# Gated one-hot rows from two ScalarE operations a token, three dense products beside each 16 tokens, and all sparse dots inside the chunks

## The reference

```python
q = (xt @ w_query).reshape(t, PEER_HEADS, 2, D_HALF)
scores = jnp.einsum('thpd,hpnd->thpn', q, sub_keys)
sv, si = lax.top_k(scores, PEER_TOPK)                  # 16 of 128, for each half of the key
...
top_s, pos = lax.top_k(cand_s, PEER_TOPK)              # 16 of the 256 sums
idx = jnp.take_along_axis(cand_i, pos, axis=-1)
gate = jax.nn.softmax(top_s, axis=-1)
...
a = jnp.einsum('ted,td->te', jnp.take(expert_u, ii, axis=0), xi)
w = gi * jax.nn.gelu(a)
y = jnp.einsum('te,ted->td', w, jnp.take(expert_v, ii, axis=0))
```

## Time and profile before

| what | value |
|---|---|
| median of the runs | 1685.22 us (1684.25 to 1688.5) |
| profiled execution | 1689.51 us, span 1687.8 us |
| mean granted TensorE clock | 0.982 |
| PE / DVE / ACT / POOL busy | 1587.2 / 1258.3 / 664.9 / 391.9 us |
| moved by DMA | 426.26 MB |

### The profile page before, as it was taken

How to read it: one execution, slowest core, us unless ns; L and a number is a source line. 1 busy time by engine, 2 the same in 40 slices (tenths; PEclk the granted TensorE clock), 3 DMA queues, 4 the chain that set the end, 5 groups by cost and what they waited for, 6 DMA issues and landing times.

```text
span 1687.8 us, 22615 instructions
## 1 busy us (share of the span) xinstructions
PE 1587.2 (94%) x7605; PEld 1292.7 (77%) x7605; DVE 1258.3 (75%) x2268; ACT 664.9 (39%) x1227; POOL 391.9 (23%) x326
## 2 busy tenths in 40 slices
PE   1899988999999999999989999799999999999995
PEld 0454465554559999999989999798888888888884
DVE  6448364439957987899788988558888878788887
ACT  2111132221337852588336853233333333333333
POOL 1101400000002320033001346413344334334420
PEclk9989989999999999999999999999999999999998
DMA  9765420000127994489736999987999999999982
GB/s 361 275 229 181 149 76 0 1 0 1 50 85 278 363 360 150 160 325 357 278 135 224 361 387 413 402 314 261 367 352 345 354 357 354 329 362 359 344 315 87
DMA packets 172770, 426.26 MB, mean 253 GB/s; under 512 B 13068, under 2 KB 62220, under 8 KB 169496
## 3 DMA queue, kind: packets, MB, share of 16 engines
q1 hardware_dynamic: 86400, 265.89, 42.2%
q0 software_dynamic: 36864, 134.23, 21.8%
q10 hardware_dynamic: 49432, 25.19, 5.3%
HBM read 372.84 MB, written 52.43 MB: 252 GB/s over the span
## 4 chain that ended last, share of the span: by engine, by line
PE 87%; DVE 6%; DMA 3%; ACT 2%; issue 1%; ACTq 1%; SPq 0%; DVEq 0%
PE bank L1152 10%; PE bank L1153 10%; PE bank L1156 10%; PE bank L1097 10%; PE bank L1099 10%; PE bank L1098 10%; PE bank L1043 7%; PE bank L951 5%; PE bank L1112 5%; PE bank L1026 3%; PE bank L961 3%; PE bank L921 1%; DMA weights<-in_w_ada 1%; PE bank L1053 1%; ACTq L842 1%
## 5 line engine op out<-in xcount | busy, mean ns | idle before, releaser
L1097 PE MATMUL bank<-h_hi,u_hi 128*128 128x384 f32 x1024 | 350.7, 343 | 22.0 <-DVE u_lo L1490 13.2
L1098 PE MATMUL bank<-h_lo,u_hi 128*128 128x384 f32 x1024 | 345.0, 337 | 0.0
L1099 PE MATMUL bank<-h_hi,u_lo 128*128 128x384 f32 x1024 | 345.0, 337 | 0.0
L1152 PE MATMUL bank<-v_hi,w_hi 128*128 128x512 f32 x768 | 299.2, 390 | 1.7 <-DVE w_lo L1597 1.6
L1153 PE MATMUL bank<-v_lo,w_hi 128*128 128x512 f32 x768 | 298.8, 389 | 0.0
L865 ACT ACTIVATE v_hi<-weights 128x1024 fp32r<-128x1024 f32 x128 | 135.8, 1061 | 330.2 <-PE bank L1156 264.3
L1156 PE MATMUL bank<-v_hi,w_lo 128*128 128x512 f32 x768 | 236.4, 389 | 0.0
L1593 DVE TENSOR_TENSOR v_lo<-weights,v_hi 128x1024 fp32r<-128x1024 f32 x128 | 157.7, 1232 | 95.2 <-ACT v_hi L865 93.0
L1490 DVE TENSOR_TENSOR u_lo<-weights,u_hi 128x1024 fp32r<-128x1024 f32 x128 | 155.9, 1223 | 95.8 <-PE bank L1099 72.7
L1097 PEld LDWEIGHTS bank<-h_hi,u_hi 128*128 128x128 f32 x1024 | 194.7, 190 | 25.3 <-DVE u_lo L1490 12.8
L1098 PEld LDWEIGHTS bank<-h_lo,u_hi 128*128 128x128 f32 x1024 | 194.8, 190 | 0.0
(11 more groups left out here) (233 smaller groups left out, 2179.6 us busy)
## 6 DMA issues: line engine op xcount, KB each, us to landing
weights<-in_uT SPq DMA_DIRECT2D x128, 512.0 KB
weights<-in_expert_v SPq DMA_DIRECT2D x128, 512.0 KB, 7.8
weights<-in_w_ada SPq DMA_DIRECT2D x12, 2048.0 KB, 10.3
gates_dense<-weights SPq DMA_DIRECT2D x24, 1024.0 KB
weights<-gates_dense ACTq DMA_DIRECT2D x16, 1536.0 KB
shared<-gelu_dense SPq DMA_DIRECT2D x64, 384.0 KB, 8.9
gelu_dense<-weights SPq DMA_DIRECT2D x32, 384.0 KB
gelu_dense<-ada SPq DMA_DIRECT2D x32, 384.0 KB
```

Source lines behind the costliest of these rows:

```text
L1097: nc.tensor.matmul(a, uh[:, k, :], h2_hi[:, :, k, :], start=(k == 0), stop=False)
L1098: nc.tensor.matmul(a, uh[:, k, :], h2_lo[:, :, k, :], start=False, stop=False)
L1099: ins = nc.tensor.matmul(a, ul[:, k, :], h2_hi[:, :, k, :], start=False, stop=(k == KC - 1))
L1152: nc.tensor.matmul(acc, wh, v_hi[:, r % 2, cols], start=begin, stop=False)
```

## The change

**Chunks.** DVE no longer makes `hot_i`. ACT makes it gated, in two operations for each token: `Square(iota128 - row number)`, and, behind a wait of ACT for its own last square, `Relu(gate - gate * square)`, which is the gate where the distance is zero and nothing elsewhere (a whole distance squared is 1 or more). The `turned` tile gets a fourth row (negated gates) and a negated first one, so ACT does three copies there for one; `iota128` moves to other columns of `ada`, and GpSimd waits for `h2_ready` before it writes them. PE waits for `hot_made` and `hot_gated` at a build.

**Products.** Each second half has two dense products: 3 a chunk for 2. After the chunks 120 products are done, and 8 stay. In the retrievals of n = 2 and 3 DVE serves the products ahead of a segment instead of behind it, by the same counts.

**Dots.** 3, 3, 3, 2 dots beside four halves in turn (5.5 a chunk), until all 128 are done. The loops behind the chunks are gone; the eight last products carry the weights of the sparse tile (`gelu` of the dots at r = 0, product with the gates at r = 2) and the first 8 adds, two a product from r = 4. In the output steps the add always stands behind L1588, and the last 8 steps have none.

**Queues.** SP issues the first loads of `v` and of the gelus behind the stores of the last tile's chunks. ACT waits for the stores of the gate matrix right behind the last chunk and issues `load_g` at r = 0 and r = 4 of the last eight products.

```diff
-LOOP_AT = 12
-DOTS_BESIDE = (4, 3)
-DOTS_IN_CHUNKS = DENSE * CHUNKS // 2 * sum(DOTS_BESIDE)
-FEW_DOTS_AT = 14
+BESIDE_HALF = (1, 2)
+LOOP_AT = 15
+DOTS_BESIDE = (3, 3, 3, 2)
+ADDS_IN_LOOP = BODY
...
+                    if n == NT - 1 and c < RAW:
+                        load_v(c, c)
+                    elif n == NT - 1:
+                        load_a(c - RAW, c - RAW)
...
             def gate_rows(half):
-                act.wait_ge(hot_made, half + 1)
...
+                if half >= HALVES:
+                    act.wait_ge(built, (half - 1) * HTOK // BATCH)
                 for q in range(HTOK):
                     token = half % (P // HTOK) * HTOK + q
+                    picked = turned[:, half * HTOK // P % 2]
                     rows = hot_i[:, half % HALVES, q, :]
-                    ins = nc.scalar.activation(rows, rows, ACT.Copy, scale=turned[:, half * HTOK // P % 2, 2, token:token + 1])
+                    ins = nc.scalar.activation(rows, iota128, ACT.Square, bias=picked[:, 0, token:token + 1])
+                ins.then_inc(hot_squared, 1)
+                act.wait_ge(hot_squared, half + 1)
+                for q in range(HTOK):
...
+                    ins = nc.scalar.activation(rows, rows, ACT.Relu, bias=picked[:, 2, token:token + 1],
+                                               scale=picked[:, 3, token:token + 1])
                 ins.then_inc(hot_gated, 1)
...
+                nc.scalar.activation(turned[:, d % 2, 0], b[:, 0:P], ACT.Copy, scale=-1.0)
+                nc.scalar.activation(turned[:, d % 2, 3], b[:, 2 * P:3 * P], ACT.Copy, scale=-1.0)
...
+                    for _ in range(BESIDE_HALF[h % HALVES] - 1):
+                        product(m)
+                        m += 1
...
-                for which, rows in ((1, hot_j), (0, hot_i)):
-                    key = turned[:, half * HTOK // P % 2, which, at:at + HTOK]
...
+                key = turned[:, half * HTOK // P % 2, 1, at:at + HTOK]
+                tt(hot_j[:, half % HALVES], iota128.unsqueeze(1).broadcast_to([P, HTOK, P]),
+                   key.unsqueeze(2).broadcast_to([P, HTOK, P]), ALU.is_equal).then_inc(hot_made, 1)
...
+                    for _ in range(BESIDE[n][segment] if n > 1 else 0):
+                        product(m)
+                        m += 1
                     next(steps, None)
...
             for r in range(BODY):
-                loop_product(ITERS - 1, r)
-                if before + BODY + r < NSEL:
-                    loop_dot(before, 1, r)
-                if r == BODY - 2:
+                if r < BODY - 1:
+                    rest_of_u(LOOP_AT, r + 1)
+                if r == 2:
                     dve.wait_ge(gelu_done, 1)
...
+                if r >= BODY // 2:
+                    for q in range(2):
+                        loop_add(-1, 2 * r - BODY + q)
```

More of the change, by code:

```diff
@@ L461, in _ @@
                 for c in range(CHUNKS):
-                    for h in range(HALVES):
+                    for _ in range(sum(BESIDE_HALF)):
                         product(m, m % BODY)
@@ L467, in _ @@
                     sp.dma_start(g_dram[g], staging[g % 2].rearrange("p i t -> p (i t)")).then_inc(g_stored[g % 2], 16)
+                    if n == NT - 1 and c == 0:
+                        wait_full(sp, "turn", DENSE - 1)
+                        for b in range(2):
+                            sp.wait_ge(a_stored[b], 16 * A_RING // 2)
+                    if n == NT - 1 and c < RAW:
+                        load_v(c, c)
+                    elif n == NT - 1:
+                        load_a(c - RAW, c - RAW)
             def loop_product(I, r, more):
@@ L853, in _ @@
                     load_g(r // RAW, r // RAW)
-                loop_product(FEW_DOTS_AT, r, True)
-            for r in range(BODY):
                 loop_product(ITERS - 1, r, False)
-                if r == BODY // 2 + 1:
+                if r == 0:
                     act.wait_ge(dot_done, NSEL)
@@ L1105, in build @@
             def build(half):
+                pe.wait_ge(hot_made, half + 1)
                 pe.wait_ge(hot_gated, half + 1)
@@ L1135, in _ @@
                     build(h)
[L1136 to L1140, removed]
+                    for _ in range(BESIDE_HALF[h % HALVES]):
+                        product(m)
+                        m += 1
+            for m in range(BODY * LOOP_AT, NKEYS):
+                product(m)
             def outputs(J, r, begin, end):
@@ L1522, in _ @@
                         rest_of_u(0, 0, True)
-                    for _ in range(BESIDE[n][segment]):
-                        product(m)
-                        m += 1
+                for _ in range(sum(BESIDE[n]) if n == 1 else 0):
+                    product(m)
+                    m += 1
                 gates(n)
@@ L1537, in _ @@
                         hot_rows(h + HALVES)
-                    product(m)
-                    m += 1
-                    for _ in range(DOTS_BESIDE[h // 2 % 2] // 2 + (h % 2 and DOTS_BESIDE[h // 2 % 2] % 2)):
+                    for _ in range(BESIDE_HALF[h % HALVES]):
+                        product(m)
+                        m += 1
+                    for _ in range(min(DOTS_BESIDE[h % 4], NSEL - dots)):
                         dve.wait_ge(gathered[dots % ROWS], 16 * (dots // ROWS + 1))
@@ L1589, in step @@
                    g_block[:, odd, :, r, :], ALU.mult).then_inc(w_made, 1)
-                if not first:
+                if adding:
                     loop_add(J, r)
```

81 lines of the change are left out of this document (28 added, 53 removed).

## The result

The changed kernel takes 1707.66 us in the median of its runs (1707.0 to 1711.14) against 1686.86 before: 1.0124 times as long, with a 95% interval of 1.0105 to 1.0143. That is 20.8 us more; 28 were forecast, with 1713 in a range of 1689 to 1727. The profiled execution has a span of 1705.8 for 1687.8, 18.0 more. One of the ten runs of the kernel of experiment 2 took 7030 us, for a cause that nothing here shows; the ratio and the differences given for that kernel are of the other nine.

The account below looks back on a forecast made before the run. PE was taken to bound the kernel, with ACT becoming the bound of the chunks. Chunks +30, retrievals +6.4, load's hold -11.1 and hand-over +2.7 sum to +28: 1717.5 us profiled, 1713 us forecast for the median, range 1689 to 1727.

Parts of the forecast that it names:

- What bounds the kernel: Whole kernel: PE's own list, from which the change takes nothing; little to win, some 22 us of waits plus clock.
- The price of the new rows: Gate rows on ACT: Square paces at 0.294 us, two-operand Relu at 0.384; a half's batch takes 5.6 us against 2.36.
- ACT as the bound of the chunks: Chunks: ACT 17.3 us against PE's 16.07, losing 1.2 a chunk and 2.8 a start; +30 us for three tiles.
- DVE's room in the chunks: Chunks: DVE's rows, `u_lo` and 5.5 dots sum to 12.8 us a chunk, so it has room.
- Retrievals: Retrievals of n = 2 and 3: products ahead of segments make PE wait 7.6 us against 5.0; +6.4 us for both.
- The term for the clock: Retrievals: 2.5 us of the old loss put down to lower clock; 0.6 more a retrieval behind four stops.
- The load's hold: Last eight products: first gate load drains in time, so the second no longer holds ACT's list; -11.1 us, bound 0.
- The hand-over: From the last products to the outputs: DVE's adds make PE wait 1.6 us, plus 1.1 of clock; +2.7 us.
- The free operand: Rival for the chunks: Relu's second operand costs nothing, +4 for +30, 1687 us; chance 0.1.
- the hidden batch: Rival at `gate_rows`: ACT's batch takes under about 4.6 us for 5.6, chunks cost 0, 1680 us; chance 0.07.
- the remaining hold: Rival at the last eight products: the load of gates still blocks, the 11.1 us stay, 1724 us; chance 0.1.
- a table load in the chunks: Rival: Square or Relu outside gelu's table forces two loads of 1.28 us a half, 122 us more, 1835; chance 0.03.

Follow-up runs that it names:

- experiment 2: Changed kernel with Relu taking a fixed scale of -1 instead of the negated gate of each partition, one copy fewer: 1685.52 us, ratio 0.9986.
- experiment 10: Kernel before the change, with the second load of gates issued later and the retrievals' segment 7 cut in two, nothing of the change: 1672.51 us, ratio 0.9909.
- experiments 2 and 3: Changed kernel with, in the first, Relu's scale fixed at -1: 1685.52 us; in the second, Square also taking a scale column of ones: 1743.37 us.
- experiment 4: Changed kernel with the row numbers' one-hot rows made by DVE again and gated by ACT in one operation a token: 1700.38 us, ratio 1.0078.
- experiment 1: Changed kernel with DVE serving the products of the retrievals of n = 2 and 3 behind each segment again: 1704.68 us, ratio 1.0106.
- experiment 7: Changed kernel with the second load of gates issued at r = 2 of the last eight products instead of r = 4: 1710.71 us, one run.
- experiment 6: Kernel before the change, with the second load of gates issued 10 products after the first instead of 4: 1681.77 us, ratio 0.9959.
- experiment 5: Changed kernel with the one-hot rows on DVE again and 2, 4, 2, 3 dots beside the halves for 3, 3, 3, 2: 1684.14 us, ratio 0.999.

## Why the prediction was right, point by point

The mechanism and the place of each term are right; all four came out nearer to zero than forecast, by 6, 1.7, 0.5 and 0.9 us, and the scatter ahead of the first build took 2.3 more off in the profile. The errors of the three costs, 8.6 us, have one sign and did not cancel, which is why 28 became 18 in the profile and 21 in the medians.

- **What bounds the kernel**: PE. Right for the kernel before; DVE's share fell from 75% to 71% of the span and PE gained nothing by it, and experiment 10 shows how little the change holds once the waits are gone on both sides.
- **The price of the new rows**: right, and tested from both sides. The relu took 0.482 us for the 0.48 reckoned, a batch 5.58 for 5.6. The sum of two operand costs read in different groups held, as the Trainium skill has it ("ScalarE: Activation LUTs", What ACT_TABLE_LOAD costs).
- **ACT as the bound of the chunks**: the mechanism is right (experiments 2 and 3), its size is off. I reckoned 17.3 us a chunk and it was 17.02, so PE loses 0.95 a chunk for 1.2: 3 x 6 x 0.25 = 4.5 of the 6 us between +30 and +24. The starts are the other 1.5: they lost 3.4, 0.9 and 2.6 us in the three tiles, for 2.8 each. The term that was too large is the rest of ACT's list: copy, gelu, copy, round pace at 2.27 us (561.85 to 564.12) where I read 2.35 from a half in which ACT had waited ahead of its copy. The wait for its own semaphore was 0.04, not 0.1, twice a chunk; no row stood behind the 0.1 or its bounds.
- **DVE's room in the chunks**: right for the changed kernel, but for a reason that I had not given. In experiment 4 a sum of 15.2 under 16.07 was no proof of room: the path from a build to a `u_lo` was 0.2 us too long, 0.6 with the hand-overs. In the changed kernel `hot_i` is off that path.
- **Retrievals**: right in kind and place (segment 7, and the turn). 7.2 us of waits in each, for 7.6 walked; +2.35 for +3.2. Experiment 1 shows it by undoing: waits of 5.5 us in each. The term for the clock was the weak one. I gave all of the 2.5 us beyond PE's recorded idle time to the lower clock and took it to grow with the number of stops. Some 0.25 us a stop is in the records themselves, and the clock behind one and the same stop took from 0 to 2.6 us (experiment 1). In the changed kernel it stayed at 1.00 behind the first stop (711.8 to 729 us) and was 0.85 behind the turn (745.8 to 757), so that the retrieval's total came out near the sum partly by luck.
- **The load's hold**: right that it goes, -10.6 for -11.1. That the first load "drains in time" was stronger than needed: in experiment 7 the issue went through with half of it moved. Taking the whole 11.1 off was right for this kernel; in experiment 6, where the traffic of before stands around the load, other waits took 2.7 of it back.
- **The hand-over**: the wait is 1.79 us, for 1.6; the clock behind it cost less than the 1.1 that I had added.
- **What I hadn't counted**: the part ahead of the first build was 2.3 us shorter in this one execution. It lies ahead of all that changed, and the first builds of the other profiles, 520.0 to 524.1, show it as the scatter of executions.
- **The rivals.** The free operand falls by the 482 ns, the hidden batch by the 5.58 us, the remaining hold by the 0.40 us; a table load in the chunks isn't there (no idle time and no load in ACT's timeline).

## What to carry to other kernels

Before work is moved from one engine to another, add up both engines' lists for a whole period, operand by operand, and compare them with the period of the engine that bounds; a move onto an engine whose list comes out 1 us a period over it costs that us every period. An average with room proves nothing by itself: walk the path from the event that an engine waits for to the value that the bounding engine needs, and move what need not be on it (one dot in experiment 5, worth 12 to 16 us). And when the bounding engine is at 94%, look at its few waits by name before the work beside it: two small edits there gave 15 us, and the change under study nothing.

## What the runs showed of the hardware

- One more operand for each partition costs an ACT operation of 128 columns 0.09 us, for `Square` and `Relu` alike: 389 to 399 ns with one, 482 to 491 with two. Where the two-operand relu read the row that it also wrote, nothing was added to that.
- An operation that waits for a semaphore of the operation just ahead on ACT started 0.04 us after that one's recorded end.
- The issue of a 1.5 MB load in 512-byte pieces was held while the load ahead of it on the same queue had much of its data to move, until 0.77 and 0.95 of 1.57 MB had gone: 2.5 us when that queue got 62% of the DMA engines' time, 15.06 us when it got 10%. In the second case ACT stood idle for 14.05 us.
- Behind the same stop of 3.44 us TensorE ran at its lower clock for 3.4, 0 and 5.6 us in three kernels (granted clock of the next 18 to 20 us 0.91, 1.00, 0.85). A stop costs 0.25 us beyond its recorded idle time even at the full clock: 0.95 lost for 0.70 recorded in the changed kernel, 0.58 for 0.32 in that of experiment 4.
